# Rotary embedding in a projection stage: the swap of half heads as a TensorE matmul, or as four 32-partition copies on ScalarE

## What is computed

```
def rope(x, pos):
    half = x.shape[-1] // 2
    ...
    x1, x2 = xf[..., :half], xf[..., half:]
    return jnp.concatenate([x1 * cos - x2 * sin, x2 * cos + x1 * sin], axis=-1).astype(x.dtype)

def nsa_project(x, pos, w_in, b_gate):
    proj = x @ w_in
    q = proj[..., :NSA_Q_COLS].reshape(B, T, NSA_HEADS, D)
    ...
    slc_kv = jnp.stack([rope(slc_kv[:, :, 0], pos), slc_kv[:, :, 1]], axis=2)
    win_kv = jnp.stack([rope(win_kv[:, :, 0], pos), win_kv[:, :, 1]], axis=2)
    gates = jax.nn.sigmoid((proj[..., NSA_GATE_OFF:] + b_gate).astype(jnp.float32)).reshape(B, T, 3, G, R)
    q_rot = rope(q, pos).reshape(B, T, G, R, D)
    return q.reshape(B, T, G, R, D), q_rot, cmp_kv, slc_kv, win_kv, gates
```

## Time and profile before

| | us |
|---|---|
| median of 3 runs | 1725.9 |
| lowest and highest run | 1719.42, 1727.41 |
| the profiled execution's own time | 1729.2 |
| its span, first to last instruction | 1727.5 |
| TensorE matmul busy in it | 1588.4 |
| VectorE, ScalarE, GpSimd busy in it | 774.2, 610.7, 754.1 |
| mean granted TensorE clock, as a share of full speed | 0.960 |

### The profile page before, as it was taken

How to read it: one execution, slowest core, us unless ns; L and a number is a source line. 1 busy time by engine, 2 the same in 40 slices (tenths; PEclk the granted TensorE clock), 3 DMA queues, 4 the chain that set the end, 5 groups by cost and what they waited for, 6 DMA issues and landing times. The chain is left out here.

```text
span 1727.5 us, 35385 instructions
## 1 busy us (share of the span) xinstructions
PE 1588.4 (92%) x13664; PEld 1399.9 (81%) x13664; DVE 774.2 (45%) x1448; ACT 610.7 (35%) x1159; POOL 754.1 (44%) x523
## 2 busy tenths in 40 slices
PE   6999567898889899999999999998998999999997
PEld 6999465566656688999999988986667999999997
DVE  2210556555556587232233276146659522223235
ACT  3221333355544436322222224136434532222322
POOL 6641663433346456544344336312136644434430
PEclk9998888799999999999999999998999999999999
DMA  8435895455375352533333222224223333233211
GB/s 242 115 84 134 270 293 173 121 182 157 119 203 168 135 182 64 183 116 115 110 123 94 78 74 69 82 91 153 85 64 112 106 99 98 82 90 104 85 33 50
DMA packets 295104, 213.39 MB, mean 124 GB/s; under 512 B 33892, under 2 KB 287384, under 8 KB 294296
## 3 DMA queue, kind: packets, MB, share of 16 engines
q1 hardware_dynamic: 277448, 178.86, 34.5%
q0 software_dynamic: 8496, 22.68, 4.1%
q10 hardware_dynamic: 8992, 9.57, 2.0%
HBM read 198.85 MB, written 20.55 MB: 127 GB/s over the span
## 5 line engine op out<-in xcount | busy, mean ns | idle before, releaser
L1801 POOL TENSOR_TENSOR w_own_t<-w_raw,w_own_t 128x1024 fp32r<-128x1024 f32 (+1 forms) x82 | 194.0, 2371 | 186.5 <-ACT w_own_t L1929 186.5
L1623 PE MATMUL ps<-x_parts,w_own_t 128*128 128x512 f32 x464 | 165.0, 396 | 3.2 <-POOL w_own_t L1801 3.2
L1801 POOL TENSOR_TENSOR w_low_ahead<-w_raw,w_high_ahead 128x1024 fp32r<-128x1024 f32 (+1 forms) x40 | 94.8, 2373 | 129.6 <-ACT w_high_ahead L1929 129.5
L1910 PE MATMUL ps<-x_parts,w_own_t 128*128 128x264 f32 x464 | 132.2, 285 | 0.0
L1912 PE MATMUL ps<-x_parts,w_own_t 128*128 128x264 f32 x464 | 131.8, 284 | 0.0
L1911 PE MATMUL ps<-x_parts,w_own_t 128*128 128x264 f32 x464 | 131.8, 284 | 0.0
L1625 PE MATMUL ps<-x_parts,w_own_t 128*128 128x256 f32 x464 | 130.1, 280 | 0.0
L1929 ACT CAST w_own_t<-w_raw 128x1024 fp32r<-128x1024 f32 (+1 forms) x82 | 83.4, 1024 | 96.4 <-PE ps L1912 80.5
L2086 DVE TENSOR_REDUCE whole_t<-ps 128x256 f32<-128x512 f32 x44 | 30.4, 690 | 181.2 <-PE ps L1625 181.2
L1163 POOL TENSOR_TENSOR e<-e,rg 128x1024 f32<-128x1024 f32 (+3 forms) x48 | 66.9, 1394 | 97.3 <-DVE rg L1433 96.7
L770 PE MATMUL ps<-flat,w 64*64 64x128 f32 (+1 forms) x2048 | 73.3, 302 | 39.2 <-DVE flat L549 20.5
(11 more groups left out here) (452 smaller groups left out, 4865.3 us busy)
## 6 DMA issues: line engine op xcount, KB each, us to landing
w_raw<-in_ffn_w_gu SPq DMA_DIRECT2D x88, 512.0 KB, 3.7
pages<-in_cache_slc SPq DMA_DIRECT2D x192, 128.0 KB
rows<-in_cache_cmp SPq DMA_DIRECT2D x116, 128.0 KB, 4.5
w_raw<-in_ffn_w_down SPq DMA_DIRECT2D x32, 448.0 KB, 3.6
w_raw<-in_gla_w_in SPq DMA_DIRECT2D x24, 512.0 KB, 3.6
rows<-in_cache_cmp POOLq DMA_DIRECT2D x84, 128.0 KB, 6.2
pages<-in_cache_slc POOLq DMA_DIRECT2D x64, 128.0 KB, 2.9
w_raw<-in_ffn_w_down SPq DMA_DIRECT2D x16, 512.0 KB, 4.0
```

What stands on the lines that cost most here:

```text
L1623: nc.tensor.matmul(bank[:, 0:2 * FOLD].rearrange("p (a n) -> p a n", a=2), high, parts[2][:, :, at, 0:FOLD], start=(k == 0), stop=False)
L1801: nc.gpsimd.tensor_tensor(low(u)[:, 0:k], raw[:, u % RAW, 0:k], high(u)[:, 0:k].bitcast(F32), ALU.subtract).then_inc(low_done, 1)
L1910: nc.tensor.matmul(psum(i), high(u)[:, k, :], a[0][:, at, c], start=(k == 0), stop=False)
```

## The change

The swap matrix, its table and its load go, and with them the swap on TensorE. ScalarE gets a step for each rotated unit, after the rounding of unit u+3: four copies of 32 partitions x 520 from `target(u)` to the rows of the other half in `by_sin`. Since `by_sin` has two buffers, these copies wait from the third on for the rotation two before. VectorE multiplies `by_sin` in place by the sines; the rest of the rotation is as it was. The two PSUM banks of the swap are not used any more in this part. GpSimd's and VectorE's waits for the tables count two loads and not three.

```
@@ phase_project
-        swap = sb("swap", [P, P])
...
@@ gpsimd
-            pool.dma_start(swap[:], io["swap_tab"]).then_inc(tab_in, 16)
...
-            pool.wait_ge(tab_in, 48)
+            pool.wait_ge(tab_in, 32)
@@ tensor
-            def swap_halves(i):
-                pe.wait_ge(raw_done, ROPED[i] + 1)
-                if i == 0:
-                    pe.wait_ge(tab_in, 48)
-                    pe.wait_ge(xT_done, 2 * NT)
-                else:
-                    pe.wait_ge(sin_done, i)
-                for hf in range(2):
-                    ins = nc.tensor.matmul(ps[:, 4 + hf, 0:HALF], swap[:], target(ROPED[i])[:, hf * HALF:(hf + 1) * HALF],
-                                           start=True, stop=True)
-                ins.then_inc(swap_done, 1)
...
-                if u - 1 in ROPED:
-                    swap_halves(ROPED.index(u - 1))
@@ scalar
+            def swap_halves(i):
+                act.wait_ge(raw_done, ROPED[i] + 1)
+                if i >= 2:
+                    act.wait_ge(rope_done, i - 1)
+                for b in range(0, P, 32):
+                    there = b ^ 32
+                    nc.scalar.copy(by_sin[there:there + 32, i % 2], target(ROPED[i])[b:b + 32]).then_inc(swapped, 1)
...
                 if u + SLOTS < NU:
                     round_high(u + SLOTS)
+                if u in ROPED:
+                    swap_halves(ROPED.index(u))
@@ vector
             def rotate(i):
-                dve.wait_ge(swap_done, i + 1)
-                if i >= 2:
-                    dve.wait_ge(rope_done, i - 1)
-                nc.vector.tensor_tensor(halves(by_sin[:, i % 2]), ps[:, 4:6, 0:HALF], halves(rope[:, 1 if i < QT else 3]),
+                dve.wait_ge(swapped, 4 * (i + 1))
+                nc.vector.tensor_tensor(by_sin[:, i % 2], by_sin[:, i % 2], rope[:, 1 if i < QT else 3],
                                         ALU.mult).then_inc(sin_done, 1)
                 dve.wait_ge(sin_done, i + 1)
                 dve.wait_ge(cos_done, i + 1)
```

More of the change, by code:

```diff
@@ L147, in phase_project @@
         high_done, low_done, proj_done, raw_done = sem("pw_high_done"), sem("pw_low_done"), sem("proj_done"), sem("raw_done")
-        swap_done, sin_done, cos_done, rope_done = sem("swap_done"), sem("sin_done"), sem("cos_done"), sem("rope_done")
+        swapped, sin_done, cos_done, rope_done = sem("swapped"), sem("sin_done"), sem("cos_done"), sem("rope_done")
         nat_done, nat_act, nat_dve = sem("nat_done"), sem("nat_act"), sem("nat_dve")
@@ L400, in _ @@
                 nc.vector.tensor_copy(xT[:, hf * 4:hf * 4 + 4, t * P:t * P + ROWS[t]], src).then_inc(xT_done, 1)
-            dve.wait_ge(tab_in, 48)
+            dve.wait_ge(tab_in, 32)
             def naturals(br):
@@ L2853, in shape_tables @@
     rope = np.concatenate([rope * np.float32(SCALE), rope], axis=1)
-    row = np.arange(P)
-    swap = (row[:, None] == np.where(row % D < half, row + half, row - half)[None, :])
     n = np.arange(SEQ // BLK)
@@ L2864, in shape_tables @@
     f = np.float32
-    return {"ropeT_tab": np.ascontiguousarray(rope), "swap_tab": swap.astype(f), "ident_tab": np.eye(P, dtype=f), "pm_01_tab": ok.astype(f),
+    return {"ropeT_tab": np.ascontiguousarray(rope), "ident_tab": np.eye(P, dtype=f), "pm_01_tab": ok.astype(f),
             "pm_add_tab": np.where(ok, f(0), f(NEG)), "mask_s_tab": np.where(own, f(0), f(NEG)),
```

## The result

The changed kernel takes 1717.05 us, median of 8 runs (1713.38 to 1721.96), the kernel before, timed beside it, 1726.59 (8 runs, 1719.42 to 1734.18). The ratio is 0.9945, 95% interval 0.9925 to 0.9965: 9.5 us less, and from 6 to 13. Forecast were 1713.4 us and 12.5 less; both intervals hold a gain of 12.5. The profiled executions have spans of 1727.5 and 1716.0 us.

A forecast was written before the change was run, and what follows sets the result against it. TensorE, busy without a gap, was taken to bound the projection; 10.4 (swaps) + 0.8 (turn 0) + 1.3 (clock) = 12.5 us off the median 1725.9 gave 1713.4 us, range 1706.5 to 1720.5.

The forecast's parts named there:

- Swaps leave TensorE: Projection: 12 swaps go from TensorE, 0.87 us each by the difference of periods 6.62 and 5.755; 10.4 us saved.
- the rival that the hand-over and not the swap costs 0.87 us: Projection: periods stay 6.62 us, total 1725.9; chance 0.18 together with the gain being taken back.
- Turn 0: First branch's transposes after unit 14: VectorE's first drain lags less, 4.46 us becomes 3.62; 0.8 saved, bounds 0 and 1.15.
- the worse of the two orders: VectorE's multiply waits for GpSimd's cosine product, 1.7 us, ending at 6.0 after the unit's copy; turn 0 loses 0.2 of 0.8.
- The clock behind turn 0: Unit 15: TensorE's clock no longer falls as turn 0's wait shrinks; 1.3 us saved, other bound 0, least certain term.
- the rival with 1714.7 us: Unit 15: the clock falls all the same, so the gain is 11.2 us; chance 0.32.
- Copies free: Projection: 48 added ScalarE copies, 0.5 us each, fit in the 4.2 us ScalarE waits for TensorE; no cost.
- ScalarE becomes the pace: Projection: above 1.08 us a copy ScalarE sets the pace, above 1.29 the kernel is slower, at most 1758 us; chance 0.06.
- The delay at SBUF: Rotated units: VectorE's multiply, now reading SBUF, and GpSimd delay each other; multiply waits 0.4 or 1.7 us, TensorE unaffected.
- The next stage takes the gain back: Compression, bound by its loads: the gain vanishes, 1725.9 us; chance 0.18 together with periods staying.
- a sign that the prediction had named as one of being wrong: Compression: a stage longer by what the projection gave would show the forecast wrong.
- The sum: Whole kernel: 10.4 + 0.8 + 1.3 = 12.5 us off, 1713.4 us from the median of 1725.9; chance 0.44.

The follow-up runs named there:

- the first profile: The kernel before, unedited, in the profiled execution that was compared with the changed kernel's; span 1727.5 us.
- the run with the cosine product first: Changed kernel, with GpSimd's cosine product of unit u put in front of its subtraction for unit u+3; 1718.01 us, one run.
- No exchange at all: Changed kernel without its ScalarE copies; VectorE multiplies the product's own rows by the sines, that part of the rotation left out; ratio 0.9927, 1715.81 us.
- the second: The kernel before, unedited, profiled once more; 1730.63 us, single run.

## Why the prediction was right

- **Swaps leave TensorE, 10.4 us.** Measured 8.67 + 1.74 = 10.41. The step from two kinds of period (6.62 and 5.755) to a price per swap held to 0.02 us, and the rival that the hand-over and not the swap costs 0.87 us fell: all periods are 5.75.
- **Turn 0, 0.8 us.** Measured 0.74 against the first profile. Against the other one, in which the clock held, 4.22 us, it is 0.50: so some 0.24 of the forecast's difference of 4.46 − 3.31 was the clock's fall, which had begun in the turn (the granted clock over turn 0 is 0.94 in the first profile and 1.00 in the other). The drain lags 111.00 − 109.94 = 1.06 us, forecast 0.95: the multiply met the cosine product, the worse of the two orders that were forecast. Without that wait, in the run with the cosine product first, turn 0 takes 3.30 us.
- **The clock behind turn 0, 1.3 us.** This is the one step that did not hold as put; that it measured 1.30 in the two profiles that were compared is luck. Of the four profiles with the same wait of 1.32 us, three of the kernel before and one with unit 13's swap on TensorE, the clock falls in two. What the change may take away is a fall that comes in some executions; the term was worth between 0 and 1.3 us in a median and should have been put somewhere between. The doubt had been stated, and the rival with 1714.7 us stood beside it; the totals can't tell 11.2 from 12.5. That a long wait plays a part is likely, since the fall is in three of the five profiles with a wait of 1.32 us or more and in none of the nine with a short one, but wait and place in time were not tried against each other, and what else decides is open.
- **Copies free.** Right, though the price was low: 0.64 us and not 0.5. The row that was taken, a copy out of PSUM, takes 0.59 us and lets the next one start after 0.49; the copies between groups of 32 partitions take 0.624 and follow each other after 0.64, their whole length. Nor did the unit's copy and rounding stay at 1.45 us: with the half-head copies in between they take 0.62 + 1.07 = 1.69. ScalarE had 1.49 us of cover left and not 2. No exchange at all gives 0.4 us more in the stage and no more than the intervals in the total.
- **ScalarE becomes the pace.** The rival was placed nearly right: at twice the copies, 1.69 + 8 × 0.64 and small gaps are 6.89 us a unit, and the gain is gone but not reversed. With 1.69 in place of 1.45 a copy would set the pace from 1.0 us on, not 1.08. At 0.64 us a copy it doesn't decide.
- **The delay at SBUF.** The prediction read the add of 2.89 us as ending when GpSimd's subtraction did. By its own rows it ended at 36.31 + 2.89 = 39.20, 0.56 us behind the subtraction (36.24 + 2.40 = 38.64), just as the multiply ends 0.56 behind the cosine product. The forecast for the worse order, a multiply that ends 6.0 us after the unit's copy, holds: it is 108.68 + 1.67 − 104.38 = 5.97 at unit 13.
- **The next stage takes the gain back.** The whole gain was not taken back: both timings keep a gain. A part of it is not shown and not excluded. The compression was 2.1 us longer in the compared profiles, a sign that the prediction had named as one of being wrong; but its length differs by 5 us between executions of one program, and together with the gate products it is as long as before. The last rotation ended 10.2 us sooner (111.08 against 121.26) and not some 12, and the projection 13.7 us sooner than in the first profile, 10.9 sooner than in the second.
- **The sum.** 12.5 forecast, 9.5 (6 to 13) and 11.7 (7 to 16) measured; the part set by the program, as the profiles show it, is 10.4 and 0.5, some 11 us, and the rest is what a fall of the clock costs where it comes. That the number came out is thus in part luck: the intervals would have taken in any gain from 7 to 13 us.

## What to carry to other kernels

Where an engine is busy without a gap, the price of an operation on it is the difference of two periods, one with it and one without, and not its booked time: here 0.87 us. Before a cost is put down to a clock or to a stage that loads set, profile the same program two or three times; a term that isn't in all of them is a chance and enters the sum as one. After the critical engine is relieved, look where its drains share two buffers: freed PSUM banks took another 2.7 us off this stage, though the total did not show it beyond doubt.

## What the runs showed of the hardware

ScalarE moves 32 partitions to another 32 at about the price of a copy of 128: 0.624 us for 520 columns, 0.64 from start to start, where a copy of 128 partitions out of PSUM takes 0.59 and lets the rounding behind it start after 0.49. Behind such moves the next rounding starts after 0.62 and no longer after 0.49, and the one after that, if no move comes between, after 0.49 again. Drains out of PSUM in between don't end this: behind turn 0 it is 0.62 where unit 13 was exchanged by copies (123.47 to 124.09 in that run) and 0.49 where it was exchanged by TensorE (115.90 to 116.39). All these cases fit one rule: an instruction doesn't overlap the one before it if it starts at another group of 32 partitions than ScalarE's last read or write of the same memory did. The rule is inferred from these times; no run tried it by itself. A VectorE multiply with both inputs in SBUF takes 0.70 us alone and 1.67 if GpSimd began an instruction that reads SBUF 0.2 us before it; GpSimd's 1.31 us are not lengthened. A swap of two float32 matmuls with 260 columns each costs a busy TensorE 0.87 us, 0.43 each; the 48 matmuls of a unit, with the same columns and operands rounded beforehand, take 5.75 us, 0.12 each. One program, with the same waits, has TensorE at 2.4 GHz over a stretch of 6.0 us in one execution and partly at 1.2 GHz, in 7.4 us, in another.
